# Prompt attentions of a hybrid decoder step: softmax reciprocals written 64 columns wide for both heads and transposed onto the output rows

## What is computed

```python
logits = jnp.einsum('ntgre,ntkge->ntgrk', qg, kv_sel[:, :, :, 0]).astype(F32) * E ** -0.5
logits = logits.reshape(N, T, H, -1) + bias
logits = jnp.where(valid[:, :, None, :], logits, NEG_BIG)
prob = jax.nn.softmax(logits, axis=-1).reshape(N, T, A_KV_HEADS, rep, -1).astype(q.dtype)
o = jnp.einsum('ntgrk,ntkge->ntgre', prob, kv_sel[:, :, :, 1])
```

## Time and profile before

| what | value |
|---|---|
| median of 3 runs | 3030.82 us |
| lowest and highest of the runs | 3025.01 and 3031.73 us |
| the profiled execution | 3019.68 us |
| its span | 3017.9 us |
| busy in the span: PE, DVE, ACT, POOL | 2887.3, 2132.7, 1015.6, 809.3 us |

### The profile page before, as it was taken

One profiled execution on the slowest core, in us unless ns is written; L12 is line 12 of the kernel. 1 busy time (PEld: TensorE's weight loads), 2 busy tenths in 40 slices (PEclk: granted clock), 3 DMA queues, 4 the chain that ended last, 5 costly groups with the idle time before them and its releaser, 6 DMA issues.

```text
span 3017.9 us, 61597 instructions
## 1 busy us (share of the span) xinstructions
PE 2887.3 (96%) x23632; PEld 2670.1 (88%) x23648; DVE 2132.7 (71%) x3723; ACT 1015.6 (34%) x1733; POOL 809.3 (27%) x882
## 2 busy tenths in 40 slices
PE   7899999998999999999989999989899999999996
PEld 6799995767999999999977999867689999999996
DVE  5699986787464444598848999867966544447888
ACT  3422113153243333343433221223333333334334
POOL 4252510001023333244341543000100333233532
PEclk9999999999999999999999999999999999999998
DMA  7343425243112222332143444443310222214222
GB/s 272 107 148 121 156 98 244 85 134 112 46 57 72 86 85 85 114 136 93 56 136 106 156 137 132 179 191 101 127 66 29 85 86 85 78 65 160 97 82 104
DMA packets 139284, 340.26 MB, mean 113 GB/s; under 512 B 20662, under 2 KB 72007, under 8 KB 135031
## 3 DMA queue, kind: packets, MB, share of 16 engines
q1 hardware_dynamic: 90050, 177.19, 16.6%
q0 software_dynamic: 33088, 102.84, 11.1%
q10 hardware_dynamic: 15844, 56.20, 5.4%
HBM read 266.11 MB, written 74.53 MB: 113 GB/s over the span
## 4 chain that ended last, share of the span: by engine, by line
PE 81%; DVE 10%; issue 3%; ACT 2%; DVEq 2%; DMA 1%; POOL 0%; SPq 0%; POOLq 0%; ACTq 0%
PE PS L1648 25%; PE PS L1194 15%; PE PS L1681 13%; PE PS L1208 5%; PE PS L1577 3%; PE PS L1039 2%; PE PS L1538 2%; PE PS L1540 2%; PE PS L1539 2%; PE PS L1118 2%; PE PS L1431 2%; PE PS L1140 1%; PE PS L1159 1%; DVE U L2763 1%; DVE U L2587 1%
## 5 line engine op out<-in xcount | busy, mean ns | idle before, releaser
L2499 DVE TENSOR_TENSOR RGR<-WS,RGR 128x512 fp32r<-128x512 f32 (+2 forms) x504 | 349.5, 694 | 280.3 <-ACT RGR L1741 279.3
L1741 ACT ACTIVATE RGR<-WS 128x512 fp32r<-128x512 f32 (+3 forms) x510 | 293.0, 576 | 526.1 <-PE PS L1648 251.9
L770 POOL TENSOR_TENSOR WS<-WS 128x512 f32<-128x512 f32 (+2 forms) x288 | 389.6, 1363 | 180.4 <-DMA WS<-wjobs 87.0
L2612 DVE TENSOR_SCALAR_CACHE_REDUCE U<-U,smu 128x384 bf16<-128x384 f32 (+5 forms) x396 | 348.5, 942 | 6.6 <-issue 0.9
L725 POOL DMA_DIRECT2D WS<-wjobs x176 | 95.0, 540 | 953.6 <-DVE RGR L2499 610.5
L1648 PE MATMUL PS<-XBR,RGR 128*128 128x264 f32 x2560 | 341.1, 284 | 1.8 <-DVE U L2510 1.1
L1741 ACT ACTIVATE U<-PS 128x528 f32<-128x528 f32 (+12 forms) x326 | 158.7, 498 | 528.3 <-PE PS L1648 229.2
L1648 PEld LDWEIGHTS PS<-XBR,RGR 128*128 128x128 f32 x2560 | 323.5, 188 | 2.6 <-issue 1.4
L1681 PE MATMUL PS<-XBR,RGR 128*128 128x264 f32 x1760 | 242.4, 284 | 0.1
L755 POOL TENSOR_TENSOR WSR<-WS,HNHR 128x1024 fp32r<-128x1024 f32 x50 | 121.1, 2428 | 413.5 <-ACT HNHR L1741 413.4
L1681 PEld LDWEIGHTS PS<-XBR,RGR 128*128 128x128 f32 x1760 | 225.6, 188 | 0.3 <-issue 0.3
(11 more groups left out here) (382 smaller groups left out, 5592.2 us busy)
## 6 DMA issues: line engine op xcount, KB each, us to landing
WS<-wjobs POOLq DMA_DIRECT2D x113, 512.0 KB, 3.8
WS<-wjobs ACTq DMA_DIRECT2D x50, 512.0 KB, 4.6
hmid<-U SPq DMA_DIRECT2D x44, 528.0 KB, 2.7
WS<-wjobs POOLq DMA_DIRECT2D x48, 384.0 KB, 3.4
Hn<-ckT SPq DMA_DIRECT2D x16, 896.0 KB, 10.8
U<-hmid SPq DMA_DIRECT2D x16, 792.0 KB, 6.6
U<-kT_pool SPq DMA_DIRECT2D x160, 64.0 KB, 1.9
xres<-U SPq DMA_DIRECT2D x2, 4224.0 KB, 16.3
```

Source lines behind the costliest of these rows:

```text
L770: pool.tensor_tensor(out=plain(p, to, g), in0=plain(p, a, g), in1=plain(p, b, g), op=op).then_inc(fw_sum, 1)
L1741: return act.activation(out, in_, ACT.Copy)
L2499: tt(out=lo, in0=plain(p, i, g), in1=hi.bitcast(F32), op=ALU.subtract).then_inc(wp_lo, 1)
L2612: ts(U[0:m, JUNK[i]:JUNK[i] + w // 2].bitcast(BF16), s, CANDF[0:m, i:i + 1], None, op, ALU.add, accum_out=into[0:m, i:i + 1])
```

## The change

VectorE now writes 1/sum 64 columns wide for each head, both heads side by side, into `DG(0)` (128 by 128), reading each sum 64 times over. TensorE turns this with one transpose, which puts head one on output rows 0 to 63 and head two on 64 to 127. There is one place for the wide reciprocals, so the reciprocal of unit `u` waits for the spread of unit `u - 1`, where it waited for that of `u - 2` before. `RC` is gone.

```diff
--- before.py
+++ after.py
@@ -307,7 +307,7 @@
             return dgt[:, u % 2, :]
 
 
-        MX, RS, RC = sm[:, 140:144], sm[:, 144:148], sm[:, 148:152]
+        MX, RS = sm[:, 140:144], sm[:, 144:148]
         WQ = sm[:, 8:44].rearrange("p (i h) -> p i h", h=4)
         WCOL = sm[:, 44:45]
         CNT, NEED, CGT = sm[:, 45:52], sm[:, 52:59], sm[:, 59:66]
@@ -1140,11 +1140,7 @@
                             mm(PS[hh * 64:hh * 64 + 64, 6, 0:P], v_at(h, j), U[:, o:o + P], start=j == 0, stop=j == i,
                                skip_group_check=True)
                     pe.wait_ge(at_rc, k * NU + u + 1)
-                    for hh in range(2):
-                        x = 2 * (u % 2) + hh
-                        m = mm(PS[hh * 64:hh * 64 + 64, 6, P:2 * P], bc(RC[:, x], 1, 64), ident, start=True, stop=True,
-                               skip_group_check=True)
-                    m.then_inc(at_pv, 1)
+                    pe.transpose(PS[:, 6, P:2 * P], DG(0), ident).then_inc(at_pv, 1)
 
                 def turn(u):
                     _, i = UNITS[k][u]
@@ -2750,9 +2746,10 @@
                         u = s - 1
                         x = 2 * (u % 2)
                         v.wait_ge(at_exp, 2 * (k * NU + u) + 2)
-                        if k * NU + u >= 2:
-                            v.wait_ge(at_pv, k * NU + u - 1)
-                        v.reciprocal(RC[:, x:x + 2], RS[:, x:x + 2]).then_inc(at_rc, 1)
+                        if k * NU + u >= 1:
+                            v.wait_ge(at_pv, k * NU + u)
+                        v.reciprocal(DG(0).rearrange("p (h e) -> p h e", h=2), bc(RS[:, x:x + 2], 2, 64)
+                                     ).then_inc(at_rc, 1)
                         for n, hh, g in mine(k, u):
                             G = k * NG + n
                             w = P * (min(4 * g + 4, UNITS[k][u][1] + 1) - 4 * g)
```

## The result

The changed kernel is slower: 3042.59 us against 3022.76 us (medians of 6 runs each; ratio 1.0069, 95% interval 1.0053 to 1.0086), 19.8 us. The forecast was slower by 36 us, at 3067. The time lies inside the stated range of 3025 to 3092, but the change was put at 1.8 times what it is, and the median it was added to, 3030.82 of three runs, came down to 3022.76 with three more.

A forecast was written before the change was run, and what follows sets the result against it. PE was taken to bound first attentions and DVE second ones: 6.3 + 12.1 - 0.5 = 17.9 us a layer, 36 in two layers, carried to the 3030.82 median as 3067 us. The range was 3025 to 3092.

The forecast's parts named there:

- The bound of each attention: In each layer's two prompt attentions, PE was taken to limit the first and DVE the second.
- the term of 1.01 us: DVE time added per unit by widening the reciprocal from 2 to 128 columns, 1168 ns in all at 8 ns a column.
- the rival of 285 ns: Wide reciprocal on DVE streams at about a copy's pace, 285 ns for 128 columns; forecast 3031 us, chance 0.22.
- The second attentions: DVE-bound: eleven units pay in full, 11.1 us, and the five before them 1.0, together 12.1 us a layer.
- The eleven steps: Eleven units of the second attention with no DVE idle time above 0.2 us, forecast to pay 1.01 us each, 11.1 together.
- the two waits named there: DVE waits of 1.00 and 0.61 us in the second attention's first five units, said to cover most of their added cost.
- The first attentions: Eight large units pay 8.1 us through PE's held fourth transpose group, less 1.8 of idle: 6.3, less 0.5 PE saving.
- That small units pay nothing: First attention's units of two groups cost nothing, covered by DVE's 14.0 us idle before reductions; without cover, up to 8.1 more.
- One place at no price: Reciprocal's wait for the previous unit's spread costs nothing extra; some 0.55 us once an attention, inside that unit's 1.01.
- PE's 0.06 us a unit: PE's saving from one transpose replacing two matmuls, the load gap staying; 0.5 us over eight large first-attention units.
- no change: Rival: wide reciprocal at about a copy's pace; DVE pays 2.8 us, PE saves 2.5; 3031 us, chance 0.22.
- faster: Rival: cheap reciprocal and PE's 0.17 us load gap gone; 13.0 less 2.8, so 10 us faster, 3021; chance 0.12.

The follow-up runs named there:

- late reciprocal: The changed kernel with the same wide reciprocal moved behind the unit's copies and the multiplication on VectorE: 3035.6 us, ratio 1.0049 to the kernel before.
- ScalarE does both: Against the kernel before, ScalarE widens narrow reciprocals for one transpose a unit and copies each unit's last transpose group in second attentions: 3023.1 us, ratio 0.9997.

## Why the prediction was right, and where it was wrong

The direction and the mechanism were right, the size was not: 36 us slower was forecast, and 19.8 measured.

- **The bound of each attention: right.** PE in the first, DVE in the second. Work moved on DVE (late reciprocal) changes the first and not the second.
- **The price of the wide reciprocal: right in kind, too high in size.** This is the step that failed: the term of 1.01 us added a unit, from a step of 8 ns a column that rested on four executions of one column and 64 of two. The step is 6.25 ns, and 0.79 us a unit were added; the term was 28% too high. With 0.79 the same sum gives 4.5 + 9.7 - 0.5 = 13.7 a layer, 27 us instead of 36. The attentions of the profiled executions show 25, so the next point takes most of the rest. The medians show 19.8 and the runs at a like granted clock 22; those last few us are of the size by which stretches outside the attentions and the clock differ from run to run, and no run splits them further. The Trainium skill ("VectorE: DVE Perf Modes", First, the fixed hardware budget) gives Reciprocal a repeat count of 8 and no cost of a column. Read as eight plain columns for one it would give the estimate of 8.4 ns, and the 6.25 ns here don't bear that reading out. The Trainium skill's other page ("Vector Engine (DVE) Microarchitecture Reference", 3.2 Anatomy of a single slice) has the divide chain span all eight slices. Read as one result a cycle it went with the rival of 285 ns, and the 948 ns refute that reading.
- **The second attentions: 12.1 forecast, 8.4 measured.** The eleven steps paid 7.3 us together, 0.66 each, from the start of the reduction of 896 columns (631.25 before, 632.79 after) to the end (681.58 and 690.37). Before, the copies there started 0.07 to 0.27 us behind the start of the reciprocal. What is above 0.07 is probably small waits for transposes, which the longer instruction now fills, so the eleven did not pay in full. The five steps ahead paid 1.1 where 1.0 was taken, but in part by luck: the two waits named there, 1.61 us together, could not cover four of the 5.05 us that five long reciprocals add by the forecast. The trace of the kernel before has more such idle time there, 0.80 and 0.45 us before reductions and 0.55 before a copy.
- **The first attentions: 6.3 - 0.5 forecast, 3.4 and 4.8 measured.** The mechanism, a fourth group held by a late first copy, is shown by the waits and by the late reciprocal. With 0.79 the sum gives 4.5 - 0.5. That small units pay nothing holds only roughly: the output of the seventh unit, the last before the first large one, is done 0.7 and 1.0 us later, counted from the first scores.
- **One place at no price: wrong with a wide reciprocal.** I had looked at the last step alone, and 0.55 us. The wait came at twelve units and cost 2 us in each first attention. It is right for a narrow one.
- **PE's 0.06 us a unit: 0.10 measured.** The gap stayed at the change of tile, as taken; but the next load starts 0.06 us behind the transpose's and not 0.105. Where the reciprocal is wide little of it is left (0.7 us between the medians with and without it, 1.3 between their attentions).
- **The base.** 36 us were carried to a median of three runs, 8 us above that of six. Of the 24 us between 3067 and 3042.59, 8 are this and 16 the price.

The rivals "no change" and "faster" both needed a reciprocal of some 0.3 us. The same spread with a cheap widening came out 3.0 us slower with a copy on VectorE and 0.6 faster with one on ScalarE, neither told apart from the kernel before, where "faster" had 10 us: of the two, "no change" would have been the nearer one.

## What to carry to other kernels

Widen a column with a copy, a matmul or another engine, and keep the reciprocal on the narrow data: each further column costs it 6.25 ns. Ask of a lengthened instruction what stands behind it on its own engine and which bank or buffer that frees; idle time elsewhere in the step covers it only if it comes before the thing that is waited for. A price taken from two points a few nanoseconds apart deserves a range as wide as the extrapolation.

## What the hardware showed that I had not expected

The reciprocal on VectorE costs 6.25 ns a column from 2 to 256 columns, while a plain copy in SBUF took 0.20 us for 64 columns and 0.23 for 128. A float32 transpose that follows matmuls of 64-column tiles (view of line 1143, duration ns min/median/max) lasts 328 ns where other transposes last 273, and still lets the next load start after 0.06 us:

```profile
L1143 PEld LDWEIGHTS PS<-CT,dgt x64: 137/138/183, 448.9 to 2187.7; 128*128 128x128 f32 x64
L1143 PE MATMUL PS<-CT,dgt x64: 327/328/477, 448.9 to 2187.7; 128*128 128x128 f32 x64
```

The place is what counts and not the operand: in the kernel before, most of the first transposes of line 1159 behind the 64-column spreads last 328 ns as well, and after the change, where line 1143 stands ahead of them, those of line 1155 mostly 273.

And runs of one kernel lay as far apart as the whole change cost: 20 us for the kernel before and 25 for the one in which ScalarE does both, with a mean granted clock from 0.985 down to 0.976. In the medians of the latter this hid a gain of some 6.7 us.
